# A hybrid decoder step on one core: the mixer is cut into two token groups, and twelve tiles of the next stage run inside the second

## The reference

```python
xn = rmsnorm(x); q, k, v, val, gate = split(xn @ w_in)          # 512 | 128 | 128 | 512 | 512 columns
A  = sliding_window_attention(rmsnorm(q), rmsnorm(k), v)        # 8 heads of 64, 2 kv heads, window 128, sinks
glu = val * sigmoid(gate)
C  = silu(layernorm(causal_depthwise_conv(glu, 31 taps))) @ pw  # 512 channels
h  = x + concat(rmsnorm(A), rmsnorm(C)) @ w_out                 # the mixer ends here
xt = rmsnorm(h)
s  = einsum(xt @ wq, keys)                  # 8 heads x 2 halves, 128 keys each
top 16 of each half, top 16 of their sums -> idx, gate = softmax            # per token and head
hu = dot(u[idx], xt);  y = h + sum(gelu(hu) * gate * v[idx])    # u, v: 16384 rows of 1024
```

## The kernel before

| stage | about, us | what is in it |
|---|---|---|
| ranking a | 409 to 484 | wqa, sca, DVE ranks |
| picks TA, TB | 484 to 559 | u tiles 0 to 16 on PE |
| ranking b | 559 to 736 | wqb, scb, ranks of 384 tokens, u tiles 17 to 32 |
| picks 0 to 2 | 736 to 889 | u tiles 33 to 68 |
| gate batches | 889 to 1265 | 64 batches of 6 tokens, u tiles 69 to 122, 152 rows |
| last u tiles | 1265 to 1293 | 5 tiles |
| v stage | 1293 to 1850 | 128 v tiles, 166 rows |

## Time and profile before

### The profile page before, as it was taken

How to read it: one execution, slowest core, us unless ns; L and a number is a source line. 1 busy time by engine, 2 the same in 40 slices (tenths; PEclk the granted TensorE clock), 3 DMA queues, 4 the chain that set the end, 5 groups by cost and what they waited for, 6 DMA issues and landing times.

```text
span 1857.0 us, 23142 instructions
## 1 busy us (share of the span) xinstructions
PE 1669.9 (90%) x8361; PEld 1449.5 (78%) x8361; DVE 1433.3 (77%) x2657; ACT 762.1 (41%) x1274; POOL 540.2 (29%) x395
## 2 busy tenths in 40 slices
PE   7888668989699998999789998999999999999997
PEld 5766446769697777999789898999877877877876
DVE  3466854238777999777899999995978888988876
ACT  3222112112352222444688887884333333333332
POOL 0000000000012333111366566662334433344330
PEclk9998887999799999999899999999999999999999
DMA  6110500125275787777699999999999999999985
GB/s 191 46 46 3 63 1 18 52 77 189 86 255 188 287 276 234 240 230 239 232 393 382 402 385 397 388 381 397 383 343 374 376 349 376 386 375 368 373 316 186
DMA packets 164360, 477.45 MB, mean 257 GB/s; under 512 B 28063, under 2 KB 61535, under 8 KB 162071
## 3 DMA queue, kind: packets, MB, share of 16 engines
q1 hardware_dynamic: 108951, 274.63, 42.6%
q0 software_dynamic: 55296, 201.35, 28.6%
HBM read 420.93 MB, written 54.42 MB: 256 GB/s over the span
## 4 chain that ended last, share of the span: by engine, by line
PE 60%; DVE 29%; issue 5%; ACT 3%; DMA 2%; SPq 0%; DVEq 0%; ACTq 0%
PE ps L782 24%; PE ps L710 17%; PE ps L523 9%; DVE ring L1348 6%; DVE lo L1233 3%; PE ps L760 3%; DVE cacc L1454 2%; DVE gA L1395 2%; DVE tsi L1245 2%; DVE tsi L1248 2%; DVE gB L1395 2%; PE ps L535 2%; DVE sm L1246 2%; DVE acc L1352 2%; DVE tsv L1247 1%
## 5 line engine op out<-in xcount | busy, mean ns | idle before, releaser
L1056 POOL DMA_INDIRECT ring<-in_u,idx x192 | 272.0, 1417 | 909.4 <-DVE ijg L1328 523.9
L1233 DVE TENSOR_TENSOR lo<-raw,hi 128x1024 fp32r<-128x1024 f32 x256 | 313.1, 1223 | 143.8 <-ACT hi L915 141.0
L915 ACT ACTIVATE hi<-raw 128x1024 fp32r<-128x1024 f32 x256 | 270.4, 1056 | 324.3 <-PE ps L782 324.3
L710 PE MATMUL ps<-xh,hi 128*128 128x384 f32 x1024 | 356.9, 349 | 27.2 <-DVE lo L1233 27.2
L1056 POOL DMA_INDIRECT ring<-in_v,idx x192 | 266.7, 1389 | 368.6 <-DVE acc L1352 354.7
L710 PE MATMUL ps<-xl,hi 128*128 128x384 f32 x1024 | 348.5, 340 | 0.0
L710 PE MATMUL ps<-xh,lo 128*128 128x384 f32 x1024 | 347.9, 340 | 0.0
L782 PE MATMUL ps<-hi,ah 128*128 128x512 f32 x768 | 239.9, 394 | 23.0 <-DVE al L1425 22.8
L1352 DVE SCALAR_TENSOR_TENSOR acc<-ring,hu,acc 128x1024 f32<-128x1024 f32 x192 | 245.5, 1279 | 1.6
L782 PE MATMUL ps<-hi,al 128*128 128x512 f32 x768 | 239.7, 394 | 0.0
L782 PE MATMUL ps<-lo,ah 128*128 128x512 f32 x768 | 239.1, 393 | 0.0
(11 more groups left out here) (176 smaller groups left out, 1972.7 us busy)
## 6 DMA issues: line engine op xcount, KB each, us to landing
raw<-in_uT SPq DMA_DIRECT2D x128, 512.0 KB, 5.9
raw<-in_v SPq DMA_DIRECT2D x128, 512.0 KB, 6.2
wring<-in_wblk SPq DMA_DIRECT2D x48, 512.0 KB, 3.5
gelu_matrix<-gest SPq DMA_DIRECT2D x64, 384.0 KB, 7.4
gate_matrix<-Gs SPq DMA_DIRECT2D x16, 1536.0 KB, 8.8
Gl<-gate_matrix SPq DMA_DIRECT2D x128, 192.0 KB, 6.6
gel<-gelu_matrix SPq DMA_DIRECT2D x128, 192.0 KB, 5.7
wring<-in_wblk SPq DMA_DIRECT2D x16, 256.0 KB, 2.5
```

What stands on the lines that cost most here:

```text
L710: mm = nc.tensor.matmul(out, a[:, n % 2, w], b[:, c, :], start=(c == 0 and k == 0), stop=(c == DC - 1 and k == 2))
L915: nc.scalar.activation(hi[:, s % 2, :], raw[:, s % RAWS, :], ACT.Copy).then_inc(s_hi, 1)
L1056: pool.indirect_dma_start(ring[:, r % SLOTS, :], None, table, bass.IndirectOffsetOnAxis(idx[:, t, c:c + 1], 0)).then_inc(g_in[r % SLOTS], 16)
L1233: nc.vector.tensor_tensor(lo[:, s % 2, :], raw[:, s % RAWS, :], hi[:, s % 2, :].bitcast(F32), ALU.subtract).then_inc(s_lo, 1)
```

## The change

- The output part of the mixer is done for two token groups, A (columns 0 to 383) and B (384 to 575, with the sample tokens). Group A has units 0 to 5; units 6 and 7 and the sample attention belong to B.
- DVE convolves blocks 0 to 2 for group A in units 1 to 3, two pieces of 8 taps in each slot (`conv_a`, one instruction of 384 columns for each tap), and for group B later, in pieces of 4 taps (`conv_b`, 128 and 64 columns for each tap).
- Group A's layernorm, `pw`, `woa`, `wob`, second norm and `xh`, `xl` follow unit 5. Then u tiles 0 to 11 run on PE between the steps of group B: units 6 and 7, sample attention, layernorm, `pwb`, `wo` (pw is loaded once more, and w_out as eight whole blocks instead of halves again). Only after that does ranking a begin.
- PSUM is planned in eight banks of 512 columns, not four pairs.
- In ranking a, low parts 12 and 13 are made after ranks 12 and 14 of 16; before, low part 0 came after all.
- Gate batches: three buffers of gA, gB and of the PSUM result (`ABUF`); DVE makes one-hots two batches ahead, ACT applies the gates of b + 1 before it copies batch b. 42 u tiles and 140 rows lie in this stage; 12 rows go to the v stage.
- SBUF is laid out anew, so that raw, hi, lo and gest exist beside the mixer's buffers.

```diff
+ABUF = 3
-U_TOP = 17
+U_MIX = 12
+U_TOP = U_MIX + 17
-V_ROW0 = B_ROW0 + 152
+V_ROW0 = B_ROW0 + 140
-CONV_AT = [0, 0, 0, 1, 2, 3, 4, 5, 6, 7, 8, 9, 10, 11, 12, 12, 12]
+CONV_AT = [0, 0, 0, 2, 4, 6, 8, 10, 12, 12, 12, 12, 12]
...
+            bank, n = use["PT5"]
+            pe.wait_ge(F[bank], n)
+            dense_u(0)
+            dense_u(1)
+            unit_transposes(6)
+            unit_scores(7)
+            dense_u(2)
+            unit_values(6)
+            dense_u(3)
+            unit_transposes(7)
+            sample_scores()
+            dense_u(4)
+            unit_values(7)
+            pe.wait_ge(s_conv_b, CC)
+            group_means("meanb", lambda k: caccb[:, k, :], CC)
+            dense_u(5)
+            sample_transposes()
+            dense_u(6)
+            group_means("varb", conv_b, CC, s_sqc, base=CC)
+            sample_values()
+            dense_u(7)
+            group_means("msAb", lambda k: mgb[:, k, :], CC, s_sqa, base=CC)
+            for m in range(CC):
+                group_gemm(f"pwb{m}", ...)
+            dense_u(8)
+            group_means("msCb", conv_b, CC, s_sqcr, base=CC)
+            dense_u(9)
+            for m in range(DC):
+                group_gemm(f"wo{m}", lambda k: mgb[:, k, :], DC, made=None if m else s_mg, base=DC)
+                if m >= 2:
+                    square_mean("ms2b", m - 2, DC, DT, GT)
+                if m == 3:
+                    dense_u(10)
+            square_mean("ms2b", DC - 2, DC, DT, GT)
+            dense_u(11)
+            square_mean("ms2b", DC - 1, DC, DT, GT)
...
             for m in range(NM):
-                if m < DC:
-                    x_low(m)
                 key_ranks("a", m, (TA, TB))
+                if m in (NM - 4, NM - 2):
+                    low(U_MIX + (m - (NM - 4)) // 2)
...
+            onehots(1)
             for b in range(NBAT):
-                if b + 1 < NBAT:
-                    onehots(b + 1)
+                if b + 2 < NBAT:
+                    onehots(b + 2)
```

More of the change, by code:

```diff
@@ L171, in hymba_peer @@
     use = {}
[L172 to L175, removed]
+    held = {}
+    after = {}
+    uses = [0] * 8
+    last = [None] * 8
+    for name, *banks in psum_plan():
+        uses[banks[0]] += 1
+        use[name] = (banks[0], uses[banks[0]])
+        held[name] = banks
+        after[name] = [n for n in {last[b]: 0 for b in banks} if n]
+        for b in banks:
+            last[b] = name
     with ExitStack() as ctx:
@@ L884, in _ @@
-            root("msC")
+                act.sem_inc(F[use[f"PT{u}"][0]], 1)
+            for u in range(CC):
+                unit_exps(u)
+                unit_transposed(u)
+                p = ready(f"glu{2 * u + 1}")
+                if u >= 2:
+                    act.wait_ge(s_glu, 2 * u - 2)
+                nc.scalar.activation(two(sg[:, u % 2, :]), two(p), ACT.Sigmoid).then_inc(s_sig, 1)
+                act.wait_ge(s_sig, u + 1)
+                act.sem_inc(F[use[f"glu{2 * u + 1}"][0]], 1)
@@ new lines, in _, with squares, swish @@
+            for u in (4, 5):
+                unit_exps(u)
+                unit_transposed(u)
+            def squares(dst, src, gate, base, made):
+                for c in range(CC):
+                    act.wait_ge(gate, base + c + 1)
+                    nc.scalar.activation(dst(c), src(c), ACT.Square).then_inc(made, 1)
+            def swish(dst, base):
+                for c in range(CC):
+                    act.wait_ge(s_ln, base + c + 1)
+                    nc.scalar.activation(dst(c), dst(c), ACT.Silu, bias=col("lb", c), scale=col("lg", c)).then_inc(s_sw, 1)
@@ new lines, in _ @@
+            merged(lambda c: mg[:, CC + c, 0:DT], lambda c: AT[:, c, :], "gc", rs[:, 1, 0:DT])
+            conv_b(12)
+            conv_b(13)
+            for m in range(1, DC):
+                attn_added(m)
+            conv_b(14)
+            conv_b(15)
+            for m in range(DC):
+                bank, n = use[f"woa{m}"]
+                dve.wait_ge(F[bank], n)
+                h_added("wob", m, 0, 0, DT)
+                if m < 6:
+                    conv_b(16 + m)
+            low(0)
@@ L1236, in key_ranks @@
+            low(11)
+            for m in range(4, DC):
+                h_added("wo", m, DC, DT, GT)
+            rstd("ms2b", rsb[:, 0, :])
+            for c in range(DC):
+                second_norm(c, DT, GT, rsb[:, 0, :])
             def key_ranks(kind, m, tiles):
```

836 lines of the change are left out of this document (503 added, 333 removed).

## The result

The changed kernel takes 1869.7 us (median of 20 runs, 1859.0 to 1878.6) against 1857.9 for the kernel before on the same chips (20 runs): ratio 1.0053, 95% interval 1.0037 to 1.0069. It is slower by half a per cent, and the forecast of 1843 is 27 us too low. The profiled execution took 1868.6 us, its span 1866.7.

The account below looks back on a forecast made before the run. PE was taken to bound the whole, idle because of others in the mixer with ranking a and in the gate batches. Terms 10 + 20.7 - 9.5 - 2 - 36 + 1 = -15.8 against 1858.8 gave 1843 us, range 1828 to 1858.

Parts of the forecast that it names:

- Units 1 to 3, +10: Early mixer: taps of 384 columns take longer than the pairs did, delaying PE by 10 us, bounds +7.5 and +14.
- Unit 4 to the query matmul, +20.7: Scores of unit 4 to first query matmul: 247.6 us instead of 226.9, bounds +8 and +38.
- the walk: PE's order followed from unit 4's scores to the first query: 220.5 us of work plus 27.1 of stalls.
- Rival 3: Mixer, group B: ACT's order becomes the bound, up to 1886 us if none of its work is covered; chance 0.08.
- Ranking a, -9.5: First query to tile 14: earlier ranking end and tiles 12 and 13 before it save 9.5 us, bounds -5 and -12.
- The chain behind the ranks: After ranking a: keyx, a table load and gelu 12 precede hi 14, so tile 14 starts 8.6 us after the ranks.
- Ranking b, -2: Ranking b to the gates' start: scores alternate two banks, transposed picks three, saving 2 us, bounds 0 and -6.
- Gate batches, -36: Gate batches: DVE's sum falls to 323 us, plus 17 of waits makes 340 instead of 376; bounds -48 and -20.
- v stage, +1: v stage: twelve more rows, 15.4 us of DVE, are nearly hidden and cost 1 us, bounds 0 and +15.4.
- The upper bound, 15.4: v stage: the largest cost allowed for the twelve added rows, +15.4 us, their DVE time.
- rival 2: Gate batches: a slower PE clock leaves a gain of 20 us instead of 36, total 1867 us; chance 0.20.

Follow-up runs that it names:

- experiment 6: Changed kernel with six instead of twelve u tiles in the mixer, without and with gate loads issued two per tile in the group before: 1841.9 and 1817.5 us.
- experiment 3: Kernel before with only the changed gate batches: three buffers, one-hots two batches ahead, gates of b + 1 before the copy of b: 1845.7 us, ratio 0.9928.

## Why the prediction was wrong

- **Units 1 to 3, +10**: right. The scores of unit 4 start at 192.33, 9.9 later.
- **Unit 4 to the query matmul, +20.7**: right in sum, 249.9 against 247.6, in part by luck: PE's work is 7.1 us over the walk, at a granted clock of 0.94, and its stalls are 4.8 under it. pw0 waited 5.9 instead of 4.4, unit 6's transposes 3.5 instead of 4.7, the first query 4.9 instead of 5.1. Rival 3 is out: ACT was in nobody's way in group B. The table loads agree with the earlier trace rows: gelu starts 1.29 us after its load begins. The 2.66 us that the Trainium skill gives for a switch (ScalarE: Activation LUTs, "What ACT_TABLE_LOAD costs") is not seen in the rows of 517.14 and 518.43.
- **Ranking a, -9.5** (its terms give -9.3): -1.2. The chain behind the ranks was right, and 2.5 us of the miss are the ranks' own. The larger part is that I took tiles 12 and 13 before the end of the ranks for a gain of waiting time and priced no slow clock after the waits that remain: behind tile 14 the stretch is 5.8 us longer than before, and PE's busy time in all 5.0. The Trainium skill (TensorE: Matmul & The Clock Gate, "HAM oscillation — how this bites in real kernels") says that waits between groups of matmuls are paid again in the clock; the 54 slow steps against 17 agree in sign, but the two six-tile kernels of experiment 6 show that the same wait is not always paid for.
- **Ranking b, -2**: nothing. Small, and the bound 0.
- **Gate batches, -36**: -37.1 in the table, -36.2 by the stretch that was forecast, with DVE's sum and waits nearly as forecast. What each part of the change gives is another matter. Three buffers alone give 10.3 (experiment 3). With them, the split mixer and the rows, but no tile moved, the stage is 381.2, 18.2 under before; the twelve tiles give the other 18.9. My terms gave the buffers nothing of DVE's time, 15.4 to the rows, 13.8 to the tiles and 7 to the waits for hi. The sum of DVE is the floor, and long stretches reach it; but how near the stage comes depends on the places of the tiles, of which nothing stood in the prediction.
- **v stage, +1**: +15.2, **the step that failed**, and more than half of the miss. The text said that PE "has waited for nothing but the changes of group" and took from it that rows between the changes are free. There they were: PE still waits nowhere between them (the eighth wait is at the start of the stage). But the term held the waits at the changes fixed, and they grew from 22.8 to 33.2 us, and PE's busy time by 4.9 at the lower clock. The waits are for the last block of the gates, which is asked for one tile ahead and takes 8.7 us to `mt` instead of 7.5 on average with twelve rows more in the stage; asked for early, it leaves the rows 4.3 us. The upper bound, 15.4, is what came, by chance: it is DVE's time for the rows in the open, and DVE's time is not what they cost. I had quoted the 22.8 us of waits and not asked what they are for; SP's queue in the trace of before shows the last load 8.4 us ahead of its use.
- **Rivals.** The time is that of rival 2 (1867), but its mechanism isn't: the gates gave 37 back at a clock of 0.94, not 20 at less. None of my cases had the rows of the v stage at their upper bound by themselves, which is where the slower outcome lay.

## What to carry to other kernels

A wait in a stage is not a constant: ask what it is for before adding work to the stage, and what that work brings with it. Here it was for a transfer asked for one tile ahead, rows with transfers of their own made it longer, and asking earlier took most of their cost away. Filling idle places with work of another stage pays only as far as there are idle places; count them (here six tiles of 4.2 us for 9.8, the next six for 21.6). And when units of work are spread over a loop that has a period of its own, lay them in that period.

## What was not expected of the hardware

- The same wait of 2.8 us was followed by six us at a granted clock of 0.50 in one kernel and of 1.00 in another that is identical in that stretch. Four short waits (14.2 us) were followed by 54 slow steps in one kernel and by about 35 in two others with the same waits, one long and one short (17.0) by 26.
- The gates' blocks of 192 KB land later when they are asked for early (median over the execution 8.4 us against 6.6 in the kernel before), and still that kernel gains 11 us: here it counts how long before its use a load is issued.
- With two tiles fewer to run, the gate stage was 18 us longer, at a clock of 0.93 instead of 0.97, for the sake of their places.
